# Two-block transformer on one core: feed-forward branch and gate in PSUM banks of their own, first tile's gate difference moved to GpSimd

## The reference, cut to what matters

```
def conv_ffn(h, w_up, conv_w, conv_b, w_down):
    u = h @ w_up
    a, b = u[..., :D_FF_2], u[..., D_FF_2:]
    a = causal depthwise convolution of width 3 over the tokens (a, conv_w) + conv_b
    return (jax.nn.gelu(a, approximate=False) * b) @ w_down

h2 = rms_norm(x, norm2_g)
x = x + conv_ffn(h2, w_ffn_up, ffn_conv_w, ffn_conv_b, w_ffn_down)
```

## Time and profile before

| | us |
|---|---|
| median of 3 runs | 1477.11 (1475.54 to 1477.27) |
| the profiled execution | 1473.65 |
| its span | 1471.9 |
| PE busy | 1393.5 (95%) |
| DVE busy | 535.4 (36%) |
| ACT busy | 341.7 (23%) |
| POOL busy | 90.3 (6%) |

### The profile page before, as it was taken

How to read it: one execution, slowest core, us unless ns; L and a number is a source line. 1 busy time by engine, 2 the same in 40 slices (tenths; PEclk the granted TensorE clock), 3 DMA queues, 4 the chain that set the end, 5 groups by cost and what they waited for, 6 DMA issues and landing times.

```text
span 1471.9 us, 23690 instructions
## 1 busy us (share of the span) xinstructions
PE 1393.5 (95%) x10108; PEld 777.6 (53%) x10108; DVE 535.4 (36%) x980; ACT 341.7 (23%) x504; POOL 90.3 (6%) x44
## 2 busy tenths in 40 slices
PE   8999999999999999899889998998999999999998
PEld 6543333333333333333333333333979999899997
DVE  1763121111211211121112111212989658777767
ACT  0531011000100110010001000101766543444452
POOL 0000000000000000000000000002000050133232
PEclk9999999999999999999999999999999999999999
DMA  9699999999999999999999999999444123255552
GB/s 360 245 395 408 429 426 428 427 429 428 428 428 428 429 429 428 428 427 428 427 428 429 428 428 428 428 429 417 167 151 158 37 82 150 95 190 187 182 197 86
DMA packets 45125, 491.38 MB, mean 334 GB/s; under 512 B 5008, under 2 KB 5520, under 8 KB 13488
## 3 DMA queue, kind: packets, MB, share of 16 engines
q1 hardware_dynamic: 44928, 490.48, 81.2%
q10 hardware_dynamic: 144, 0.13, 0.0%
HBM read 489.54 MB, written 1.05 MB: 333 GB/s over the span
## 4 chain that ended last, share of the span: by engine, by line
PE 66%; DMA 28%; DVE 3%; ACT 2%; POOL 0%; issue 0%; SPq 0%; DVEq 0%; ACTq 0%
DMA ring<-in_w_exp 20%; PE bank L841 16%; PE bank L870 10%; PE bank L898 8%; PE bank L899 8%; PE bank L900 8%; DMA work<-in_w_exp 5%; DMA spare<-in_w_exp 3%; PE bank L800 3%; PE bank L788 2%; PE bank L729 2%; PE bank L650 1%; PE bank L680 1%; PE bank L808 1%; ACT spare L1487 1%; PE bank L861 1%
## 5 line engine op out<-in xcount | busy, mean ns | idle before, releaser
L841 PE MATMUL bank<-ring,spare 128*64 128x512 f32 x1344 | 302.2, 596 | 23.7 <-DMA ring<-in_w_exp 23.4
L2016 DVE TENSOR_SCALAR work<-bank 128x512 f32<-128x512 f32 x32 | 22.1, 691 | 740.5 <-PE bank L841 740.5
L841 PEld LDWEIGHTS bank<-ring,spare 128*64 128x64 f32 x1344 | 92.7, 136 | 219.8 <-issue 160.5
L870 PE MATMUL bank<-ring,spare 128*64 128x512 f32 x672 | 148.8, 595 | 14.7 <-ACT spare L1487 14.7
L899 PE MATMUL bank<-work_parts,ring_parts 128*128 128x256 f32 x568 | 158.1, 278 | 0.0
L1483 ACT ACTIVATE work<-work 128x512 f32<-128x512 f32 x32 | 20.2, 631 | 535.5 <-DVE work L2016 535.5
L841 PE MATMUL bank<-work,spare 128*64 128x512 f32 x576 | 129.7, 595 | 9.7 <-DMA work<-in_w_exp 9.7
L899 PEld LDWEIGHTS bank<-work_parts,ring_parts 128*128 128x128 f32 x568 | 107.0, 188 | 1.1
L870 PEld LDWEIGHTS bank<-ring,spare 128*64 128x64 f32 x672 | 46.9, 137 | 103.1 <-issue 90.3
L898 PE MATMUL bank<-hn_hi,ring_parts 128*128 128x256 f32 x352 | 98.1, 279 | 0.0
L900 PE MATMUL bank<-hn_hi,ring_parts 128*128 128x256 f32 x352 | 96.5, 274 | 0.0
(11 more groups left out here) (467 smaller groups left out, 1982.3 us busy)
## 6 DMA issues: line engine op xcount, KB each, us to landing
ring<-in_w_exp SPq DMA_DIRECT2D x126, 2048.0 KB, 34.6
work<-in_w_exp SPq DMA_DIRECT2D x54, 2048.0 KB, 34.9
spare<-in_w_exp SPq DMA_DIRECT2D x12, 2048.0 KB, 31.4
ring<-in_ffn_up SPq DMA_DIRECT2D x22, 1024.0 KB, 4.9
ring<-in_ffn_down SPq DMA_DIRECT2D x22, 512.0 KB, 3.5
ring<-in_w_in SPq DMA_DIRECT2D x2, 2048.0 KB, 17.2
ring<-in_w_out SPq DMA_DIRECT2D x4, 1024.0 KB, 16.7
ring<-in_w_k SPq DMA_DIRECT2D x4, 1024.0 KB, 16.5
```

Source lines behind the costliest of these rows:

```text
L841: ins = pe.matmul(to[n2 * CAP:(n2 + 1) * CAP, :], x_e[:, 2 * j + kk, :], w[:, b, kk, n2 * BANK:(n2 + 1) * BANK], start=False, stop=j == UP ...
L870: ins = pe.matmul(y_bank[n2 * CAP:(n2 + 1) * CAP, :], hidT[:, k % 4, k // 4 * CAP:(k // 4 + 1) * CAP], w[:, kk, n2 * BANK:(n2 + 1) * BANK] ...
L2016: dve.tensor_scalar(gt, bank[4][:, :], LIMIT, None, ALU.min).then_inc(gt_ready, 1)
```

## The change

The branch of a tile goes to bank 4 + i and the gate to bank 6 + i, and `ffu_used[i]` counts twice for each tile, after the branch and after the gate. VectorE's `convolve` waits for the first count and `hidden` for the second; ScalarE's cast up waits for the second. The last transposed quarter goes to bank 7 in place of bank 6. The first `ffn_up(1)` writes its gate into bank 7, so `ffn_up(1)` waits ahead of its gate until `rms_row` has been copied out.

The first tile's up difference is split: VectorE does the branch half (128x1024), counting `rest_second` to 2; GpSimd then does the gate half (128x1024), counting `up_rest[0]`. The first `ffn_up(0)` waits for each half where it needs it. GpSimd then waits for `x_rest` 11 before its two first `down_part`.

```
-            TAIL_BANK = {(0, 0): 6, (1, 0): 7, (0, 1): 5, (1, 1): 6}
+            TAIL_BANK = {(0, 0): 6, (1, 0): 7, (0, 1): 5, (1, 1): 7}
 (ffn_up, TensorE)
-                pe.wait_ge(up_rest[i], use)
+                if first:
+                    pe.wait_ge(rest_second, 2)
+                else:
+                    pe.wait_ge(up_rest[i], use)
...
-                    ins = three_passes(bank[4 + i][:, c * T:(c + 1) * T], [a[:, c, k, :] for a in w], (hnT_hi2[k], hnT_rest[:, k, :]),
-                                       c == 0 and k == 0, k == KD - 1)
-                ins.then_inc(ffu_used[i], 1)
+                    if first and c == 1 and k == 0:
+                        pe.wait_ge(up_rest[i], use)
+                    if i == 1 and c == 1 and k == 0:
+                        pe.wait_ge(split_ready, 4 + 4 + 1 + 1 + 1)
+                    ins = three_passes(bank[4 + 2 * c + i][:, 0:T], [a[:, c, k, :] for a in w], (hnT_hi2[k], hnT_rest[:, k, :]),
+                                       k == 0, k == KD - 1)
+                    if k == KD - 1:
+                        ins.then_inc(ffu_used[i], 1)
 (next_part, ScalarE)
-                act.wait_ge(ffu_used[i] if cols is up_cols else ffd_used[i], now)
+                if cols is up_cols:
+                    act.wait_ge(ffu_used[i], act.snap(now * 2))
+                else:
+                    act.wait_ge(ffd_used[i], now)
 (first tile, VectorE)
-            dve.tensor_tensor(ff_rest[0][:, 0:2 * D], ff_land[0][:, 0:2 * D], ff_hi[0][:, 0:2 * D].bitcast(F32), ALU.subtract).then_inc(up_rest[0], 1)
+            dve.tensor_tensor(ff_rest[0][:, 0:D], ff_land[0][:, 0:D], ff_hi[0][:, 0:D].bitcast(F32), ALU.subtract).then_inc(rest_second, 1)
 (convolve, hidden, VectorE)
-                dve.wait_ge(ffu_used[i], now)
+                dve.wait_ge(ffu_used[i], dve.snap(now * 2 - 1))
...
-                g = bank[4 + i][:, T:2 * T]
+                g = bank[6 + i][:, 0:T]
+                dve.wait_ge(ffu_used[i], dve.snap(now * 2))
 (GpSimd)
             pool.wait_ge(mm_ready, 14)
+            pool.wait_ge(ff_upper[0], 1)
+            pool.wait_ge(rest_second, 2)
+            pool.tensor_tensor(ff_rest[0][:, D:2 * D], ff_land[0][:, D:2 * D], ff_hi[0][:, D:2 * D].bitcast(F32), ALU.subtract).then_inc(up_rest[0], 1)
+            pool.wait_ge(x_rest, 7 + 4)
             for i in range(2):
                 down_part(i, 2)
```

More of the change, by code:

```diff
@@ L2510, in turned @@
                 dve.wait_ge(hT_done, 7 + 2 * b + t + 1)
-                dve.tensor_tensor(hnT[:, 4 * b:4 * b + 4, t * P:(t + 1) * P], bank[{(0, 0): 6, (1, 0): 7, (0, 1): 5, (1, 1): 6}[t, b]][:, :].rearrange("p (k t) -> p k t", k=4),
+                dve.tensor_tensor(hnT[:, 4 * b:4 * b + 4, t * P:(t + 1) * P], bank[{(0, 0): 6, (1, 0): 7, (0, 1): 5, (1, 1): 7}[t, b]][:, :].rearrange("p (k t) -> p k t", k=4),
                                   wide(col2("norm2_g_2")[:, 4 * b:4 * b + 4], P), ALU.mult).then_inc(hT_ready, 1)
```

## The result

The changed kernel takes 1481.11 us (median of 20 runs, 1477.27 to 1484.47) against 1477.14 (20 runs, 1475.54 to 1478.45): ratio 1.0025, 95% interval 1.0019 to 1.0031. It is slower by some 4.0, outside the range that was given. Its runs scatter over 7 us, those of the kernel before over 3 here, but over 5.6 to 6.8 in the later series, so the scatter by itself says little.

What follows compares the result with a forecast made beforehand. The prediction took TensorE's own rate to bound the loop. It summed -1.35 at the last tile and +1.14 at the second to -0.2, a median of 1476.9 us, range 1474.4 to 1479.3.

Steps and rivals of the forecast that it cites:

- The end: Last tile: `convolve`'s chain starts earlier, so the last `ffn_down(1)` no longer waits; gain 1.35 us.
- The loop gains and loses nothing from the banks: Loop of 22 tiles: separate banks and two counts change nothing, 0; bound 2.6 us either way.
- The first tile's difference and the gate half on GpSimd: First tile: VectorE free about 1.07 us earlier but gain 0; gate half on GpSimd done in time, cost 0.
- The down halves behind `x_rest` 11: Second tile: GpSimd's first down half holds off L2542, so TensorE's second `ffn_up` starts late; loss 1.14 us.
- rival C: Second tile: VectorE's `norm` (L2040) is held by GpSimd too; loss 1.82, net +0.5, 1477.6 us; chance 0.08.
- B: Second tile: both GpSimd down halves get in ahead of L2542; loss 3.48, net +2.1, 1479.2 us; chance 0.10.
- the port rule: SBUF: VectorE two-input or two-port instructions and GpSimd SBUF reads hold a port pair throughout, first come first served.

Runs made afterwards that it cites:

- e2: Changed kernel's banks, counts and waits, but the first tile as in the kernel before (no gate half on GpSimd): 1473.62 us, ratio 0.9976.
- e3: Kernel before's banks and one count per tile, with the changed first tile only (split difference, gate half, wait for `x_rest`): 1483.70 us, ratio 1.0046.
- e4: Changed kernel with GpSimd's down halves waiting for `up_rest[1]`, VectorE's second-tile up difference, in place of `x_rest` 11: 1474.58 us, ratio 0.9990.
- e1: Changed kernel without GpSimd's wait for `x_rest` 11, so its down halves run as soon as their casts allow: 1475.45 us, ratio 0.9986.
- e5: Changed kernel with GpSimd's down halves waiting for `hn_ready` 4 in place of `x_rest` 11: 1478.11 us, ratio 1.0014.
- e7: Changed kernel, its wait for `x_rest` 11 kept, with the two scaled diagonals (L2053) on ScalarE instead of VectorE: 1476.60 us, ratio 0.9996.
- e8: Changed kernel with useless matmuls filling TensorE's two waits at the second tile, `keep_warm` n = 2 and 1: 1478.52 us, ratio 1.0012.
- e6: Changed kernel with useless matmuls in TensorE's two waits at the second tile, `keep_warm` n = 4 and 3: 1478.74 us, ratio 1.0016.

## Why the prediction was wrong

*The end*: right. 1.35 forecast, 1.52 in the profile; the 0.17 more is the restart after an idle time (1465.64 to 1465.95) and a `ffn_down` of 2.76. e2 and e3 show it with and without.

*The loop gains and loses nothing from the banks*: right. VectorE's wait at `convolve` was the last tile's alone, and the new banks show both steps (8.35 in e4, 8.47 in e1). The longer step of the profile is no part of the change: the kernel before has it too. 2.4 of the 6.2 between the two profiles is chance. A hint stood in the table of times: the profiled execution of before was 3.46 under its own median.

*The first tile's difference and the gate half on GpSimd*: right, cost and gain 0. The third residual add now waits 0.71 for TensorE.

*The down halves behind `x_rest` 11*: here the step failed. The mechanism, two engines that exclude each other, is shown by e1, e4, e5 and e7, but the size is 5.2 to 5.3 and not 1.14, for two reasons. First, I took L2040 for a form that is not held, because its 128 columns take as long as the cast's 256. It is held. That was rival C, and I priced it with the port free after the first operation. But the first L2053 gives GpSimd's second operation the next turn, the second L2053 waits for that, and L2555 comes last: C and B together, 3.64. That B's price of 3.48 lies near is luck: B has L2542 lose a turn, and it lost none. My argument against B, that a waiting VectorE gets its turn, was right (e5), but VectorE spent that turn on 128 columns. By the Trainium skill ("VectorE: DVE Perf Modes", The perf-mode tier table), which gives such a `tensor_scalar` the two-port mode, it would be held by the port rule that the prediction gives; the trace agrees (2.46), and I had weighed the rule as unlikely. The trace of before could have warned me, for it has a `tensor_scalar` of one column as well:

```profile
1283.24 0.20 DVE L2506 TENSOR_SCALAR work<-work 128x1 f32<-128x1 f32 x1
```

From it to L2040's 0.29 the 127 further columns take 0.09, an estimate of 0.7 ns each, where a `tensor_tensor`'s take (0.69 - 0.42) / 256 = 1.05 ns. So L2040 goes at a faster rate than a `tensor_tensor`, and its 0.29 is mostly a fixed part; to compare its duration with a cast's said nothing of its form.

Second, I let TensorE resume at full clock after an idle time. The prediction has no term for that; it is 1.66 against the first profile, 1.51 against the one with the same step of the loop, and e8's second `ffn_up` gets it back.

The sum with the measured terms: 3.64 + 1.66 - 1.52 = 3.8, against 4.0 and 3.8 measured. That it agrees so well is in part luck. The same reckoning meets e1, e4, e7 and e8 within 0.4, but e2 is 2.2 below it, e6 2.9 below, e5 1.5 above, and e3 1.2 above even with a fall of the clock counted in. What moves whole runs by that much is open; the terms are shown by the starts in the profiles, not by the medians.

*What beats both*: e1, e2 and e4 keep the banks and give GpSimd no large operation while VectorE is urgent. e2 has the lowest ratio, 0.9976; the intervals of e1 and e2 overlap, those of e2 and e4 too, so which is best is not settled.

## What to carry to other kernels

Before work goes to GpSimd, or is given a later start there, list every VectorE instruction that can come within its duration, small ones too, and let the queues alternate: here two small held instructions let two large ones in. An engine whose deadline has 0.06 to spare is no place for a new neighbour. A wait of TensorE costs its length and, when it is long (2.7 here) or two come close together, perhaps a stretch at half clock; and a profile that lies 3 us under its own median should be taken again before another is compared with it.

## What the runs showed of the hardware that was not expected

- A VectorE `tensor_scalar` of 128 columns in float32, SBUF to SBUF, takes 0.29 alone and 2.2 to 2.5 beside a GpSimd `tensor_tensor`. A reciprocal of one column took 0.15 alone, and again at 1287.89, just behind the start (1287.84) of GpSimd's second operation; none was seen further inside one.
- TensorE's clock went to 0.50 for about 3.4 us (reckoned from the granted clock of the stretches) after two waits of 1.83 and 1.49 with four matmuls between them, in three of four profiles with these waits, and in none with a single wait of 1.1 or 2.0 or with the waits filled. In the experts' part it fell after a single wait of 2.74 and 2.76 (e1, e3) and not after one of 1.25 (the other eleven).
- The matmuls of the loop run in one of two steady steps, 8.35 or 8.47 a tile (`ffn_up` 5.55 or 5.71, `ffn_down` 2.80 or 2.76), in one and the same program. Of thirteen profiles five had the shorter one. The first `ffn_up` takes 5.6 in eleven profiles, of either kind (before 1282.76 to 1288.38, before again 1282.89 to 1288.51), so the longer step sets in within the part and is not there from its start. It goes neither with the banks nor with the clock's fall alone; what sets it stays open.
